# Transposed input, first two blocks interleaved, and the retention's rotation moved to VectorE, in a two-layer block on one core

## The reference, cut to what matters

```python
proj = x @ w_in[l]                                  # (256 x 1024) @ (1024 x 2560)
q, k, v, g, p = jnp.split(proj, ...)                # 512 columns each
q = _rope(q.reshape(b, s, RET_HEADS, RET_HEAD_DIM)) # 4 heads of 128
k = _rope(k.reshape(...)) * (RET_HEAD_DIM ** -0.5)
ret = _retention(q, k, v)                           # scores q k^T times decay, times v
...
pool = _pool_mixer(p, w_pool[l], pool_scale[l])
mix = jnp.concatenate([ret, pool], axis=-1) @ w_out[l]
x = _layernorm(DEEPNORM_ALPHA * x + mix, ln1_g[l], ln1_b[l])

def _rope(t):                                       # cos, sin by token and feature
    t1, t2 = tf[..., : dh // 2], tf[..., dh // 2:]
    return jnp.concatenate([t1 * cos - t2 * sin, t1 * sin + t2 * cos], axis=-1)
```

## Time and profile before

| | |
|---|---|
| median of 3 runs | 1063.96 us (1062.73 to 1064.88) |
| the profiled execution | 1064.28 us |
| its span, first to last instruction | 1062.2 us |
| granted TensorE clock, mean | 0.998 |
| busy: PE, DVE, ACT, POOL | 1053.3, 744.6, 596.0, 96.6 us |
| HBM read and written | 214.71 MB, 17.83 MB |

### The profile page before, as it was taken

How to read it: one execution, slowest core, us unless ns; L and a number is a source line. 1 busy time by engine, 2 the same in 40 slices (tenths; PEclk the granted TensorE clock), 3 DMA queues, 4 the chain that set the end, 5 groups by cost and what they waited for, 6 DMA issues and landing times.

```text
span 1062.2 us, 13204 instructions
## 1 busy us (share of the span) xinstructions
PE 1053.3 (99%) x5110; PEld 885.3 (83%) x5110; DVE 744.6 (70%) x870; ACT 596.0 (56%) x800; POOL 96.6 (9%) x73
## 2 busy tenths in 40 slices
PE   9999999999999999999999999999999999999997
PEld 7888888888888888888888888888989988888886
DVE  5668788784787676467986778758768666867642
ACT  6463676764385645448754545562455557555531
POOL 1900000000000000000454600010000000000000
PEclk9999999999999999999999999999999999999999
DMA  9755999985587777565447755568955346787741
GB/s 353 284 194 161 300 303 284 297 274 184 188 276 236 244 234 237 180 208 189 159 159 235 239 160 172 185 250 264 314 187 193 119 145 217 232 245 241 243 165 39
DMA packets 157294, 233.41 MB, mean 220 GB/s; under 512 B 9856, under 2 KB 99888, under 8 KB 157104
## 3 DMA queue, kind: packets, MB, share of 16 engines
q1 hardware_dynamic: 153808, 221.16, 64.7%
q0 software_dynamic: 3136, 11.23, 3.1%
q10 hardware_dynamic: 288, 0.20, 0.1%
HBM read 214.71 MB, written 17.83 MB: 219 GB/s over the span
## 4 chain that ended last, share of the span: by engine, by line
PE 91%; DVE 4%; ACT 2%; DMA 2%; issue 1%; SPq 1%; DVEq 0%; ACTq 0%
PE ps L825 21%; PE ps L826 21%; PE ps L824 21%; PE ps L863 5%; PE ps L861 5%; PE ps L862 5%; PE ps L958 2%; PE ps L1275 1%; PE ps L1277 1%; PE ps L1276 1%; PE ps L1158 1%; DVE rest L1963 1%; DMA x<-in_x_dram 1%; DMA mem_blocked<-mem_turned 1%; ACT high L1393 1%
## 5 line engine op out<-in xcount | busy, mean ns | idle before, releaser
L1963 DVE TENSOR_TENSOR rest<-raw,high 128x2048 fp32r<-128x2048 f32 x131 | 307.4, 2362 | 83.6 <-ACT high L1393 83.1
L824 PE MATMUL ps<-high,xt_high 128*128 128x512 f32 x840 | 330.4, 393 | 0.0
L826 PE MATMUL ps<-high,xt_rest 128*128 128x512 f32 x840 | 327.0, 389 | 0.0
L825 PE MATMUL ps<-rest,xt_high 128*128 128x512 f32 x840 | 327.0, 389 | 0.0
L1393 ACT ACTIVATE high<-raw 128x2048 fp32r<-128x2048 f32 x131 | 248.4, 1913 | 67.6 <-DMA raw<-in_ffn_w_down_dram 33.0
L826 PEld LDWEIGHTS ps<-high,xt_rest 128*128 128x128 f32 x840 | 157.7, 188 | 33.0
L824 PEld LDWEIGHTS ps<-high,xt_high 128*128 128x128 f32 x840 | 157.8, 188 | 31.6
L825 PEld LDWEIGHTS ps<-rest,xt_high 128*128 128x128 f32 x840 | 157.8, 188 | 31.4
L1968 DVE SCALAR_TENSOR_TENSOR rest<-raw,wgain,high 128x512 fp32r<-128x512 f32 x176 | 119.1, 747 | 35.8 <-ACT high L1397 35.8
L1397 ACT ACTIVATE high<-raw,wgain 128x512 fp32r<-128x512 f32 x176 | 110.9, 716 | 9.6 <-DMA raw<-in_ffn_w_in_dram 9.6
L1655 ACT ACTIVATE act<-ps,recips 128x256 f32<-128x256 f32 x44 | 18.5, 471 | 85.0 <-PE ps L826 85.0
(11 more groups left out here) (372 smaller groups left out, 1481.5 us busy)
## 6 DMA issues: line engine op xcount, KB each, us to landing
raw<-in_w_in_dram SPq DMA_DIRECT2D x88, 512.0 KB, 4.5
raw<-in_ffn_w_in_dram SPq DMA_DIRECT2D x88, 512.0 KB, 4.8
raw<-in_w_up_dram SPq DMA_DIRECT2D x44, 512.0 KB, 5.3
raw<-in_ffn_w_down_dram SPq DMA_DIRECT2D x44, 512.0 KB, 4.3
raw<-in_w_down_dram SPq DMA_DIRECT2D x22, 512.0 KB, 4.5
raw<-in_w_out_dram SPq DMA_DIRECT2D x16, 512.0 KB, 5.5
raw<-in_w_mkv_dram SPq DMA_DIRECT2D x16, 512.0 KB, 5.6
gv_turned<-gv_blocked SPq DMA_DIRECT2D x11, 512.0 KB, 5.3
```

The costliest lines, as they stand in the source:

```text
L824: pe.matmul(out, sh, wh, start=first, stop=False)
L825: pe.matmul(out, sh, wr, start=False, stop=False)
L826: mm = pe.matmul(out, sr, wh, start=False, stop=last)
L1963: vec.tensor_tensor(rest[:, slot, c], raw[:, slot, c], high[:, slot, c].bitcast(F32), ALU.subtract).then_inc(unit_rest, 1)
```

## The change

1. `x` is also passed by features (`x_t`, laid out so that each DMA reads one contiguous stretch) and loaded in five parts (`XT_PARTS`, slices 0, 1, 2-3, 4-5, 6-7), the first on ACT's queue. ScalarE and VectorE split it straight from SBUF. The 16 transposes of x and their groups in PSUM are gone. `x` by tokens is loaded later, as one DMA of 1 MB after unit 9, for the first residual sum.
2. The first four units are now q and k crosswise: units 0 and 1 are the first half of the features of q and of k, 2 and 3 the second half. They come in twelve pieces (`LEAD_PIECES`) and TensorE takes q and k slice by slice.
3. All weights are laid out in HBM unit by unit, each DMA one contiguous stretch (4 KB a partition for a 512 KB DMA) in place of rows of 1, 2 or 4 KB.
4. Units 4 and 5 are held back until lead pieces 8 and 10 have landed, units 6 and 7 until units 4 and 5 have. GpSimd's constants wait for lead piece 7 (the rotary tables) and for unit 4 (the others).
5. VectorE rotates q and k instead of GpSimd, and transposes them in 32x32 squares; SP turns them through HBM (`turn_rotated`, inside `load(9)` and `load(10)`). q's turned form is read by the scores as it lies, k's is put in order by a copy on ScalarE. The 16 transposes on TensorE and four evictions are gone.
6. The warm-up is 7 matmuls in place of 6 and 4, on a smaller zero tile.

```diff
+WARM = 7
+LEAD_UNITS = 4
+LEAD_BEFORE = {4: 8, 5: 10}
+XT_PARTS = ((0, 1), (1, 2), (2, 4), (4, 6), (6, 8))
+LEAD_PIECES = tuple((j, k, k + 1) for k in range(4) for j in range(2)) + tuple((j, k, k + 2) for j in range(2) for k in (4, 6))
...
# SP
+            def load(u):
...
+                if u in LEAD_BEFORE:
+                    sync.wait_ge(lead_landed[LEAD_BEFORE[u]], 16)
                 if u >= SLOTS:
                     sync.wait_ge(unit_used, u - SLOTS + 1)
+                if u in (SLOTS, SLOTS + 1):
+                    sync.wait_ge(unit_landed[u - 2], 32)
+                for n in range(2):
+                    c = slice(2 * n * NB, 2 * (n + 1) * NB)
+                    sync.dma_start(raw[:, slot, c], piece("units", u * 4 * NB + c.start, u * 4 * NB + c.stop)).then_inc(unit_landed[slot], 16)
+                turn_rotated(u)
...
+            def turn_rotated(u):
+                n = u - UNIT["win1"] - 9
+                if not 0 <= n < 2:
+                    return
+                sync.wait_ge(rot_blocked, n + 1)
+                sync.dma_start(rot_turned[n], rot_home(n)).then_inc(rot_stored, 16)
+                sync.wait_ge(rot_stored, 16 * (n + 1))
+                src = rot_turned[n].rearrange("(q i) (r e) -> r i q e", q=4, r=4)
+                dst = rk[:, :, :].rearrange("p t c -> p (t c)") if n else rot_home(n)
+                for r in range(4):
+                    sync.dma_start(dst[32 * r:32 * r + 32, :].rearrange("p (q e) -> p q e", q=4), src[r]).then_inc(rot_landed[n], 16)
...
+            for u in range(LEAD_UNITS, UNIT["end"]):
+                load(u)
+                if u == UNIT["wout1"] - 1:
+                    sync.dma_start(x[:, :, :], dram["x"].rearrange("(t p) c -> p t c", p=P)).then_inc(x_landed, 16)
# TensorE
+            for n, (j, k0, k1) in enumerate(LEAD_PIECES):
...
+                if n == 0:
+                    pe.wait_ge(xt_first, 1)
+                    pe.wait_ge(lead_high, 1)
+                    for tt in range(TT):
+                        xh, _, wh, _, out = lead(0, tt)
+                        pe.matmul(out, xh, wh, start=True, stop=False)
+                pe.wait_ge(lead_rest, n + 1)
+                if j == 0:
+                    pe.wait_ge(xt_rests, [part for part, (x0, x1) in enumerate(XT_PARTS) if x0 <= k0 < x1][0] + 1)
+                for k in range(k0, k1):
+                    for tt in range(TT):
+                        xh, xr, wh, wr, out = lead(k, tt)
+                        if n:
+                            pe.matmul(out, xh, wh, start=(k == 0), stop=False)
+                        pe.matmul(out, xh, wr, start=False, stop=False)
+                        mm = pe.matmul(out, xr, wh, start=False, stop=(k == KC - 1))
+                if k1 % 4 == 0:
+                    mm.then_inc(unit_used, 1)
+            full_block("win1", 2)
...
-            rotated_transposes(0, "q", rq)
             half_block("win1", 3, 0)
-            rotated_transposes(1, "k", rk)
...
-            wait_taken(("rTq", 0), ("rTq", 1), ("rTk", 0), ("rTk", 1))
+            pe.wait_ge(rot_landed[0], 64)
+            pe.wait_ge(sem("rk_turned"), 1)
# ScalarE
             for j, dst in enumerate((stage[:, 0, :, :], stage[:, 1, :, :], rp[:, :, :])):
                 split_to(UNIT["win1"] + 2 * j + 4)
                 take_block("win1", j, dst)
-            for g in range(2):
-                take(("rTq", g), rqT[:, 2 * g:2 * g + 2, :])
             split_to(UNIT["win1"] + 9)
-            for g in range(2):
-                take(("rTk", g), rkT[:, 2 * g:2 * g + 2, :])
+            act.wait_ge(rot_landed[1], 64)
+            act.activation(rkT[:, :, :, :].rearrange("p t h (q i) -> p (t h) q i", q=4),
+                           rk[:, :, :]..., ACT.Copy).then_inc(sem("rk_turned"), 1)
             for g in range(2):
                 take(("poolT", g), pooled[:, 2 * g:2 * g + 2, :])
             split_to(UNIT["win1"] + 10)
# VectorE
+            def rotate(j, dst):
+                vec.wait_ge(rope_landed, 32)
+                vec.wait_ge(pair_taken[j], taken("win1", j)[1])
...
+                for tt in range(TT):
+                    c4 = ropec[:, tt, :].unsqueeze(1).to_broadcast([P, RH, P])
+                    vec.tensor_tensor(d4[:, tt], s4[:, tt], c4, ALU.mult).then_inc(rotated, 1)
+                    for half in range(2):
...
+                        vec.tensor_tensor(a4[:, tt, :, o], s4[:, tt, :, i], sn, ALU.mult).then_inc(rotated, 1)
+                vec.wait_ge(rotated, 3 * TT * (j + 1))
+                vec.tensor_tensor(dst[:, :, :], dst[:, :, :], ra[:, :, :], ALU.add).then_inc(sem("rope_done"), 1)
+
+            def squares(j, rows):
+                vec.wait_ge(sem("rope_done"), j + 1)
+                vec.transpose(rot_home(j)..., rows...).then_inc(rot_blocked, 1)
+
+            split[0] = LEAD_UNITS
+            split_to(UNIT["win1"] + 5)
+            rotate(0, rq)
+            squares(0, rq)
+            split_to(UNIT["win1"] + 6)
+            rotate(1, rk)
+            squares(1, rk)
             split_to(UNIT["win1"] + 10)
```

More of the change, by code:

```diff
@@ L542, in _, with load_xt, load_lead @@
         def _(sync):
[L543 to L559, removed]
+            def load_xt(n):
+                k0, k1 = XT_PARTS[n]
+                sync.dma_start(xt_raw[:, k0:k1, :], piece("x_t", k0 * S, k1 * S).rearrange("p (k t) -> p k t", t=S))\
+                    .then_inc(xt_landed[n], 16)
+            def load_lead():
+                for n, (j, k0, k1) in enumerate(LEAD_PIECES):
+                    u = 2 * (k0 // 4) + j
+                    c = slice((k0 % 4) * NB, ((k1 - 1) % 4 + 1) * NB)
+                    for part, (x0, _) in enumerate(XT_PARTS):
+                        if part and j == 0 and x0 == k0:
+                            load_xt(part)
+                    at = u * 4 * NB
+                    sync.dma_start(raw[:, u, c], piece("units", at + c.start, at + c.stop)).then_inc(lead_landed[n], 16)
+            def load(u):
                 slot = u % SLOTS
+                if u in LEAD_BEFORE:
+                    sync.wait_ge(lead_landed[LEAD_BEFORE[u]], 16)
                 if u >= SLOTS:
                     sync.wait_ge(unit_used, u - SLOTS + 1)
-                for dst, src in parts(raw[:, slot, :]):
-                    sync.dma_start(dst, src).then_inc(unit_landed[slot], 16)
+                if u in (SLOTS, SLOTS + 1):
[4 more added lines that the diff above has]
+                turn_rotated(u)
                 turn_conv(u)
@@ L651, in load_up @@
[L651 to L663, removed]
@@ L1012, in _ @@
-            mm.then_inc(unit_used, 1)
-            wait_taken(("x", 1), ("x", 3))
-            tiles = [chunk_products("win1", 0, 1, tt) for tt in range(TT)]
-            for k in range(4):
-                pe.wait_ge(*((sem("lead_rest"), k + 4) if k < 3 else (unit_rest, 2)))
-                for tt in range(TT):
-                    sh, sr, c, out, first, last = tiles[tt][k]
-                    wh, wr = high[:, 1, c:c + NB], rest[:, 1, c:c + NB]
-                    pe.matmul(out, sh, wh, start=first, stop=False)
-                    pe.matmul(out, sh, wr, start=False, stop=False)
-                    mm = pe.matmul(out, sr, wh, start=False, stop=last)
@@ new lines, in input_rest @@
+            def input_rest(n):
+                k0, k1 = XT_PARTS[n]
+                vec.wait_ge(*((xt_highs, n) if n else (xt_first, 1)))
+                vec.tensor_tensor(xt_rest[:, k0:k1, :], xt_raw[:, k0:k1, :], xt_high[:, k0:k1, :].bitcast(F32), ALU.subtract)\
+                    .then_inc(xt_rests, 1)
+            vec.wait_ge(xt_landed[0], 16)
+            vec.tensor_copy(xt_high[:, 0, :], xt_raw[:, 0, :]).then_inc(xt_first, 1)
+            input_rest(0)
+            for n, (j, k0, _) in enumerate(LEAD_PIECES):
+                for part, (x0, _) in enumerate(XT_PARTS):
+                    if part and j == 0 and x0 == k0:
+                        input_rest(part)
+                weights_rest(n)
@@ L2168, in _ @@
             split_to(UNIT["up1"] + 2)
+            vec.wait_ge(x_landed, 16)
             half_stats("wout1", 0, 0)
@@ L2741, in _, with in_pieces @@
             assert split[0] == UNIT["end"]
+def in_pieces(rows, ends):
+    return np.concatenate([rows[:, a:b].ravel() for a, b in zip([0] + list(ends), ends)])
 def constants():
```

262 lines of the change are left out of this document (114 added, 148 removed).

## The result

The changed kernel takes 1072.16 us (median of 4 runs, 1071.07 to 1074.35), the one before 1063.88 beside it (4 runs, 1062.73 to 1064.88): ratio 1.0084, 95% interval 1.0071 to 1.0098. It is 8.3 us slower, where 1063.2 was forecast in a range of 1060.4 to 1065.8. The profiled execution took 1072.69 us, its span 1070.8 against 1062.2.

What follows compares the result with a forecast made beforehand. TensorE, busy 1053.3 of 1062.2 us, was taken as the bound. Terms -3.1 - 1.7 + 3.7 + 0.1 + 0.4 = -0.6, rounded to 0.7 less, took 1063.96 to 1063.2 us; range 1060.4 to 1065.8.

Steps and rivals of the forecast that it cites:

- What bounds the kernel: Whole kernel: TensorE, busy 1053.3 of 1062.2 us; gains only from the start, fewer TensorE instructions and the memory's small wait.
- Start: Blocks q and k: first matmuls at 4.7 us, blocks ending at 27.95 instead of 31.08, 3.1 us earlier.
- T: Time of q's last matmul in the opening blocks, taken as 22.3 us, bounds 21.5 and 23.5.
- Transposes: Rotated q and k on TensorE: two groups of eight, 0.87 us each, fall away; 1.7 us less.
- VectorE's detour: Rotating and turning q and k delays units 5 and 6 by 1.8 us each; together 3.7 us, bounds 3.6 and 5.0.
- The sum: Total of all terms: -3.1 - 1.7 + 3.7 + 0.1 + 0.4 = -0.6 us, rounded to 0.7 less.
- What VectorE gets back: Splits slowed during GpSimd's rotation return 6.6 us of VectorE time, worth nothing by itself; units 7 to 9 in time.
- The turn through HBM: Before the scores: keys ready at T+31.5, due at T+32.9; wait put at 0.4 us, between 0 and 2.4.
- Loads: Longer runs, held-back weights: no gain, as TensorE waits for no weight; scores' queries in short runs also nothing, at most 0.9 us.
- The memory's wait: TensorE's 0.9 us wait for the memory's turned rows in the kernel before, expected at best to shrink.
- The keys come late: Rival, chance 0.14: store and reads queue behind megabytes, scores wait 3.6 us instead of 0.4; 1066.4 us.

Runs made afterwards that it cites:

- the run with the rests first: Changed kernel with VectorE's order alone changed: remaining splitting of units 4 and 5 before rotating and turning q, of unit 6 before k; 1072.67 us, ratio 1.0087.
- with gains and x late: Changed kernel with GpSimd's three gain loads held until k is in order and x's 1 MB load issued after unit 11; 1065.18 us, ratio 1.0011.

## Why the prediction was wrong, step by step

- **What bounds the kernel**: right. TensorE's waits, with the slow pace behind one, tell all but 0.6 us of the loss.
- **Start**: right in kind, 1.2 us too small. The first product at 4.49 (4.7 forecast); the usual pitch from 5.63 us on, where I had kept the 7.0 of before; no landing was waited for. T came out at 21.1, outside my bounds of 21.5 to 23.5, and -4.3 stands in place of -3.1. Why the clock rose earlier was not tried alone; TensorE had been busy with 128x512 matmuls from 1.06 us, where it had begun at 1.46 before.
- **Transposes**: -1.7 is taken over into the account; no run priced them alone.
- **VectorE's detour**: right, 1.6 and 1.8 us of waiting for 1.8 and 1.8. The sum added it to what came behind; the run with the rests first shows that in the changed kernel it lies beside the longer way of the keys instead.
- **What VectorE gets back**: right, the rests go at 2.2 us. I gave GpSimd's earlier idleness no price, and it has one: its gain loads, 10 us earlier, cost about 3 us.
- **The turn through HBM: here the prediction failed.** "The store is queued on SP behind q's reads, a 1 MB load of x and unit 10, so it goes out at about T+18.7" took q's store as landed by then. It took 8.8 us, not 5.3, and with it and the issues behind it k's store went out at T+23.5, 4.8 us late. Then "A store lands after 5.3 us (2.8 to 7.6)": 12.3, 7.0 more. Reads and copy were 2.2 us quicker than forecast. The keys were ready at T+41.1 against T+31.5, beyond my bound of T+35.3, and due at T+33.1 (32.9 forecast): 8.1 us of waiting where I had 0.4. The fault is where the price was taken from: later turns. In the kernel before, ten of the eleven gv_turned stores go out 1.4 to 2.4 us after the last unit's first DMA, with nothing else in between, and land in 5.3 us by the median although the DMA engines are busy 96 to 99% of that stretch. Here unit 9 stands ahead of q's store, issued 4.8 us earlier and landed only at about 39.4, and 2.5 MB of q's reads, x and unit 10 ahead of k's, with 1.5 MB of gains beside them on GpSimd's queue; the engines move 330 GB/s while it is out, 4.1 MB in all. A store's time is then about the time of the bytes that were put out before it. My own rows had 415 GB/s only for 20 to 30 us, and I used them for "the queues ran full" but not to divide the bytes by.
- **After the wait**: no term at all for the clock. The scores' slow pace cost 1.8 us.
- **Loads**: right; nothing waits for a weight. The memory's wait of 1.6 us is of this execution: of the twelve experiments one shows it at all, with 0.4, so I leave it out of the change's price.
- **The rivals**: "The keys come late" (0.14) is what happened, with a size of 3.6 us for 8.1. Its first half, the store behind x and unit 10, is what the trace shows, though at 5 us where the store took 12.3: it left out the gains, q's reads and the store's own bytes, and that q's store would be late the same way. Its second half, the reads behind another megabyte, did not come: the last took 2.9.

What stays open: with gains and x late, k's store still took 8.9 us behind unit 10 alone. That it lands behind unit 10 is shown; why q's reads and unit 10 went at only 252 GB/s between 44 and 50 us is not. Nor is it shown what ScalarE's queue is worth apart from the earlier moment.

## What to carry to other kernels

Price a DMA by what is outstanding when it is issued, not by the median of its kind: count the megabytes ahead of it on its queue, those on the other queues, and every wait that the issuing engine takes on the way. A round trip through HBM needs its store issued before any wait or load that can come later, and cover for store, reads and copy together; moving it to another engine's queue frees the first engine, and its loads then run beside the reads. When an engine is relieved, look at what it issues next and when; and add to a wait of several microseconds on TensorE what the clock takes afterwards.

## What the runs showed of the hardware

- A 512 KB store issued right behind unit 10 on SP's queue landed in 12.3 us, 1.3 us after the unit. Issued before unit 10 on ScalarE's queue it landed in 3.4 us, and 6.9 us after unit 10 on SP's queue in 3.8.
- Four reads of 128 KB landed in 2.5 to 2.9 us while SP was held back, and in 8.3 to 11.3 us with SP's loads beside them.
- After waits of 8.0 and 4.0 us TensorE resumed at half pace (8 transposes in 1.76 instead of 0.88 us); after 2.9 us it did not. The price was 1.8 and 2.5 us beside the wait itself.
